# Attention outputs kept as features by tokens, two heads at a time, with probabilities scaled before they are turned

## What is computed

```python
# block 1, fox: 8 heads, causal, with a forget bias per query and key
s = einsum('qhd,khd->hqk', q, k) * scale + c_q - c_k
p = softmax(where(causal, s, -inf));  o_f = einsum('hqk,khd->qhd', p, v)
# block 1, swa: 8 heads on 2 key heads, rotary, window 128, one sink per head
p = softmax(concat([where(band, s, -inf), sink]))[..., :-1]
merged = g_f * (o_f @ w_proj_fox) + g_s * (o_s @ w_proj_swa)
# then an MoE with 64 experts (w1, w3, w2), and block 2:
# layer 0: gMLP mixer and 4 heads over 256 memory tokens; layer 1: moba (12 heads,
# here plain causal attention, as 256 tokens are one block) and 4 memory heads
x = layer_norm(ALPHA * x + concat([mix, mem_out]) @ w_mix_out)
x = layer_norm(ALPHA * x + swiglu(x))
```

## Time and profile before

| | us |
|---|---|
| median of 3 runs | 1712.14 |
| lowest and highest run | 1710.25, 1712.56 |
| span of the profiled execution | 1709.9 |
| PE busy | 1344.7 |
| DVE busy | 617.3 |
| ACT busy | 418.7 |

### The profile page before, as it was taken

One profiled execution on the slowest core, in us unless ns is written; L12 is line 12 of the kernel. 1 busy time (PEld: TensorE's weight loads), 2 busy tenths in 40 slices (PEclk: granted clock), 3 DMA queues, 4 the chain that ended last, 5 costly groups with the idle time before them and its releaser, 6 DMA issues.

```text
span 1709.9 us, 20307 instructions
## 1 busy us (share of the span) xinstructions
PE 1344.7 (79%) x8918; PEld 916.5 (54%) x8918; DVE 617.3 (36%) x821; ACT 418.7 (24%) x569; POOL 10.0 (1%) x64
## 2 busy tenths in 40 slices
PE   8999877686655656565665556689999999999998
PEld 8999724142212212221221222159888889898886
DVE  5667401001100100110011001047866676776665
ACT  5754400000000000000000000045544435444441
POOL 2000000000000000000000000000000000000000
PEclk9999989888877887877887878789999999999999
DMA  9545899999999999999999999994556655345560
GB/s 297 182 158 206 343 418 427 429 426 428 426 428 429 427 428 427 428 428 428 427 428 425 426 428 426 421 306 162 199 174 196 210 184 173 106 166 177 192 213 34
DMA packets 132233, 540.07 MB, mean 316 GB/s; under 512 B 8528, under 2 KB 90800, under 8 KB 108080
## 3 DMA queue, kind: packets, MB, share of 16 engines
q1 hardware_dynamic: 132128, 538.76, 79.6%
q10 hardware_dynamic: 16, 0.00, 0.0%
HBM read 537.69 MB, written 1.05 MB: 315 GB/s over the span
## 4 chain that ended last, share of the span: by engine, by line
PE 51%; DMA 36%; DVE 5%; ACT 4%; SPq 3%; issue 2%; DVEq 0%; ACTq 0%
DMA big<-in_w_dram 35%; PE bank L1768 9%; PE bank L2101 8%; PE bank L104 7%; PE bank L106 7%; PE bank L105 7%; PE bank L1797 4%; PE bank L2102 4%; SPq L95 3%; ACT hi_b L321 1%; DVE lo_b L335 1%; PE bank L1113 1%; PE bank L592 1%; PE bank L555 1%; PE bank L1730 1%
## 5 line engine op out<-in xcount | busy, mean ns | idle before, releaser
L1768 PE MATMUL bank<-big,xe 128*32 128x512 f32 x1984 | 284.4, 737 | 251.6 <-DMA big<-in_w_dram 251.6
L1768 PEld LDWEIGHTS bank<-big,xe 128*32 128x32 f32 x1984 | 78.1, 132 | 456.0 <-issue 456.0
L335 DVE TENSOR_TENSOR lo_b<-raw_b,hi_b 128x2048 fp32r<-128x2048 f32 x90 | 205.6, 2291 | 105.9 <-ACT hi_b L321 105.9
L1860 DVE TENSOR_TENSOR x<-bank,x 128x512 f32<-128x512 f32 x60 | 41.5, 692 | 530.1 <-PE bank L1712 530.1
L2101 PE MATMUL bank<-xT,hi_b 128*128 128x512 f32 x576 | 204.3, 398 | 0.0
L321 ACT CAST hi_b<-raw_b 128x2048 fp32r<-128x2048 f32 x91 | 172.8, 1904 | 20.4 <-PE bank L106 20.4
L1797 PE MATMUL bank<-big,gT 128*32 128x512 f32 x936 | 132.2, 716 | 54.7 <-DMA big<-in_w_dram 54.7
L2102 PE MATMUL bank<-xT,lo_b 128*128 128x256 f32 x576 | 161.7, 281 | 0.0
L2101 PEld LDWEIGHTS bank<-xT,hi_b 128*128 128x128 f32 x576 | 108.2, 188 | 26.4
L1797 PEld LDWEIGHTS bank<-big,gT 128*32 128x32 f32 x936 | 36.6, 128 | 135.9 <-issue 135.9
L2102 PEld LDWEIGHTS bank<-xT,lo_b 128*128 128x128 f32 x576 | 108.8, 189 | 0.6
(11 more groups left out here) (338 smaller groups left out, 2174.6 us busy)
## 6 DMA issues: line engine op xcount, KB each, us to landing
big<-in_w_dram SPq DMA_DIRECT2D x190, 2048.0 KB, 20.5
raw_b<-in_w_ffn_in_dram SPq DMA_DIRECT2D x44, 1024.0 KB, 5.1
raw_b<-in_w_ffn_out_dram SPq DMA_DIRECT2D x22, 1024.0 KB, 5.1
raw<-in_w_in_dram SPq DMA_DIRECT2D x15, 1024.0 KB, 9.9
raw_b<-in_b_w_in_dram SPq DMA_DIRECT2D x10, 1024.0 KB, 5.1
raw_b<-in_w_mix_out_dram SPq DMA_DIRECT2D x8, 1024.0 KB, 5.1
raw_b<-in_a_w_in_dram SPq DMA_DIRECT2D x7, 1024.0 KB, 12.8
raw<-in_w_out_dram SPq DMA_DIRECT2D x4, 1024.0 KB, 5.1
```

Source lines behind the costliest of these rows:

```text
L335: dve.tensor_tensor(self.lo[i % NRAW], self.raw[i % NRAW], self.hi[i % NH].bitcast(F32), ALU.subtract).then_inc(*self.s_lo.up(i))
L1768: last = pe.matmul(hb.t[32 * e:32 * e + 32, :], xe[:, k, 32 * e:32 * e + 32], each[e][k // 4][:, k % 4 * 512:(k % 4 + 1) * 512], start=(k ...
```

## The change

The values are the weights now (128 keys by 64 features), and the turned probabilities move (128 queries). An even head's output goes to partitions 0 to 63 and the odd head's to 64 to 127 of the same columns, in turns, so that the bank holds the output as features by tokens. The transposes of the outputs and their buffers are gone. As queries are columns there, the reciprocal of the sum can't be applied behind; instead ACT multiplies each head's probabilities (queries on partitions) by it, before PE turns them. The values are done for two units at a time, at step u+4 of the first, so the buffers of turned probabilities are 4 instead of 2. The output's bank is kept until ACT and DVE have read it. A reciprocal is taken per unit; the sink's Exp and sum too. Block 1 and block 2 use the same semaphores. Both kernels have the same score, mask, Exp and transpose instructions. Cut to its core:

```diff
 def pe_attend(pe, ps, a, ident, fill):
...
-            pe.wait_ge(*a.s_exps.of(a.base + u))
+            pe.wait_ge(*a.s_scaled.of(a.base + u))
             for i in range(0, n, P):
                 last = pe.transpose(b.t[:, i:i + P], a.p[u % 4][:, i:i + P], ident[:, :])
             last.then_inc(*a.s_p_turned.up(a.base + u))
         for go in fill.get(step, ()):
             go()
-        for job, k in a.ripe(step):
...
-            for i in range(nh // 2):
-                last = pe.transpose(b.t[:, i * P:(i + 1) * P], a.o[n % 2][:, i * P:(i + 1) * P], ident[:, :])
-            last.then_inc(*a.s_o_turned.up(n))
-        if 0 <= step - 3 < len(a.units):
-            u = step - 3
...
-                for kt in range(job.nkt):
-                    at = i * job.width + kt * P
-                    last = pe.matmul(o, a.pt[u % 2][:, at:at + P], job.value(h, kt), start=(kt == 0),
-                                     stop=(kt == job.nkt - 1))
+        if a.pair_at(step - 4):
+            two = a.pair_at(step - 4)
...
+            pe.wait_ge(*a.s_p_out.of(a.base + two[-1]))
+            each = [(h, a.pt[u % 4], i * job.width) for u in two for i, h in enumerate(a.units[u][1])]
+            for side in zip(*([x for x in each if x[0] % 2 == odd] for odd in range(2))):
+                for kt in range(job.nkt):
+                    for h, pt, at in side:
+                        last = pe.matmul(o[rows64(h % 2), h // 2 * P:(h // 2 + 1) * P], job.value(h, kt),
+                                         pt[:, at + kt * P:at + (kt + 1) * P], start=(kt == 0), stop=(kt == job.nkt - 1))
+            last.then_inc(*a.s_value.up(*(a.base + u for u in two)))
+        for u in a.ripe(step):
+            ps.let(("o", a.out_at[a.units[u][0].name]))

 def act_attend(act, ps, a, fill):
...
             last.then_inc(*a.s_exps.up(a.base + u))
+        for u in a.pair_at(step):
+            job, hs = a.units[u]
+            act.wait_ge(*a.s_share.of(a.base + u))
+            for i, h in enumerate(hs):
+                row = a.p[u % 4][:, i * job.width:(i + 1) * job.width]
+                last = act.activation(row, row, ACT.Identity, scale=job.rc[:, h:h + 1])
+            last.then_inc(*a.s_scaled.up(a.base + u))
         for go in fill.get(step, ()):
             go()

 def dve_attend(dve, ps, a, fill):
...
-            if a.base + u >= 2:
-                dve.wait_ge(*a.s_value.of(a.base + u - 2))
-            dve.tensor_copy(a.pt[u % 2][:, 0:n], ps.of(("p", a.base + u))[:, 0:n]).then_inc(*a.s_p_out.up(a.base + u))
+            if a.base + u >= 4:
+                dve.wait_ge(*a.s_value.of(a.base + u - 4))
+            dve.tensor_copy(a.pt[u % 4][:, 0:n], ps.of(("p", a.base + u))[:, 0:n]).then_inc(*a.s_p_out.up(a.base + u))
+        for u in a.pair_at(step):
+            job, hs = a.units[u]
+            sm, rc = job.sm[:, picked(hs)], job.rc[:, picked(hs)]
+            dve.wait_ge(*a.s_exps.of(a.base + u))
+            if job.sinks is not None:
+                dve.tensor_tensor(sm, sm, rc, ALU.add).then_inc(*a.s_masked.up(("sum", a.base + u)))
+                dve.wait_ge(*a.s_masked.now())
+            dve.reciprocal(rc, sm).then_inc(*a.s_share.up(a.base + u))
         for go in fill.get(step, ()):
             go()
...
-            dve.reciprocal(rc, job.sm).then_inc(*a.s_masked.up(("rc", a.base + u)))
...
-                dve.tensor_tensor(a.o[n % 2][:, 0:nh * 64].rearrange("p (h d) -> p h d", h=nh),
-                                  ps.of(("o", n))[:, 0:nh * 64].rearrange("p (h d) -> p h d", h=nh),
-                                  rc[:, h0:h0 + nh].unsqueeze(2).broadcast_to([P, nh, 64]), ALU.mult).then_inc(
-                                      *a.s_o_out.up(n))

 # ripe(step): the job's last unit u with max(u + 4, hold) == step (before: max(u + 5 + late, hold),
 # at most the number of units + 4); an extra last step is gone
 # sp_first
-        sp.wait_ge(*s["o_turned"].of(self.mix.n_out - 1))
 # act_first, fillers of fox and swa: the sigmoids go from step 11 to step 12
-        fill.update({5: [rotated], 11: [sigmoids], 13: [split], 15: [split]})
+        fill.update({5: [rotated], 12: [sigmoids], 13: [split], 15: [split]})
 # pe_last, fillers of the last attention: the second projection part goes from step 19 to step 17
-        fill.update({13: [lambda: memory_part(0)], 15: [lambda: memory_part(1)], 16: [first], 19: [first]})
+        fill.update({13: [lambda: memory_part(0)], 15: [lambda: memory_part(1)], 16: [first], 17: [first]})
```

More of the change, by code:

```diff
@@ L38 @@
 WM = 768
-PER_BANK = 8
 N_ROUNDS = S // CAP
@@ L527, in last, with pair_at, picked @@
         return hs is job.units[-1]
+    def pair_at(self, step):
+        two = range(step, min(step + 2, len(self.units)))
+        return two if step % 2 == 0 and step >= 0 else ()
     def ripe(self, step):
[L531 to L536, removed]
+        return [u for u in range(len(self.units)) if self.last(u) and max(u + 4, self.hold) == step]
+def picked(hs):
+    return slice(hs[0], hs[-1] + 1, hs[1] - hs[0])
 def pe_attend(pe, ps, a, ident, fill):
-    for step in [*a.steps(), len(a.units) + 4]:
+    for step in a.steps():
         if step % 2 == 0 and step < len(a.units):
@@ L600, in act_attend @@
[L600 to L619, removed]
+        if a.pair_at(step - 4):
+            two = a.pair_at(step - 4)
+            job = a.units[two[0]][0]
+            n = a.out_at[job.name]
+            if n not in job.opened:
+                job.opened[n] = ps.take(("o", n), a.s_o_lo, n, hold=True)
+                pe.wait_ge(*job.opened[n].was)
+            o = job.opened[n].t
+            pe.wait_ge(*a.s_p_out.of(a.base + two[-1]))
[6 more added lines that the diff above has]
+            last.then_inc(*a.s_value.up(*(a.base + u for u in two)))
@@ new lines, in pe_attend, with act_attend @@
+        for u in a.ripe(step):
+            ps.let(("o", a.out_at[a.units[u][0].name]))
+def act_attend(act, ps, a, fill):
+    for step in a.steps():
+        for u in a.pair_at(step):
+            job, hs = a.units[u]
+            nh, w = len(hs), job.width
+            p3 = a.p[u % 4][:, 0:nh * w].rearrange("p (h k) -> p h k", h=nh)
+            src = p3
+            if job.mask is None:
+                src = ps.of(("score", a.base + u))[:, 0:nh * w].rearrange("p (h k) -> p h k", h=nh)
+            act.wait_ge(*a.s_peak.of(a.base + u))
+            if u >= 4:
+                act.wait_ge(*a.s_p_turned.of(a.base + u - 4))
+            for i, h in enumerate(hs):
+                last = act.activation(p3[:, i, :], src[:, i, :], ACT.Exp, bias=job.nm[:, h:h + 1],
+                                      scale=SCALE if job.mask is None else 1.0, accum_out=job.sm[:, h:h + 1])
+            if job.sinks is not None:
+                act.wait_ge(*a.s_sink.of(a.base + u))
+                last = act.activation(job.rc[:, picked(hs)], job.rc[:, picked(hs)], ACT.Exp)
+            last.then_inc(*a.s_exps.up(a.base + u))
+        for u in a.pair_at(step):
[5 more added lines that the diff above has]
+            last.then_inc(*a.s_scaled.up(a.base + u))
@@ L620, in act_attend @@
         for go in fill.get(step, ()):
             go()
-        for job, k in a.ripe(step):
-            h0, nh = job.groups[k]
-            n = a.out_at[job.name, k]
+        for u in a.ripe(step):
+            job, _ = a.units[u]
+            n = a.out_at[job.name]
             h3, _ = pair(job.put.dst)
-            act.wait_ge(*a.s_o_turned.of(n))
-            act.copy(h3[job.put.at(h0, nh, job.qt)], ps.of(("o turned", n))[:, 0:nh * 64].rearrange(
+            act.wait_ge(*a.s_value.of(a.base + u))
+            act.copy(h3[job.put.at(0, job.heads, job.qt)], ps.of(("o", n))[:, 0:job.heads * 64].rearrange(
@@ L680, in dve_attend @@
                 dve.wait_ge(*signal.of(point))
[L681 to L701 removed]
+            dve.tensor_tensor(l3[at], ps.of(("o", n))[:, 0:job.heads * 64].rearrange("p (c s) -> p c s", s=P),
+                              h3[at].bitcast(F32), ALU.subtract).then_inc(*a.s_o_lo.up(n, (job.name, 0)))
 class Program:
```

137 lines of the change are left out of this document (49 added, 88 removed).

## The result

The kernel after takes 1719.28 us (median of 4 runs, 1717.19 to 1721.65), beside 1712.35 for the kernel before on the same chip: ratio 1.0042, 95% interval 1.003 to 1.0054. It is slower by 6.9 us, more than the 0.2% that a measurement can tell. Run once more later it took 1721.6 us beside 1711.2, ratio 1.006 (1.0043 to 1.0077). The prediction was 1717.2, slower.

A forecast was written before the change was run, and what follows sets the result against it. PE was taken to bound the attentions, a DMA stream the expert stage. Fox/swa -0.5, memory 0 +2.2 and memory 1 plus moba +3.4 gave +5.1 us on a 1709.9 span: 1715.0, so 1717.2 in whole time; range 1706 to 1723.

The forecast's parts named there:

- PE work: All attentions: 13.3 us saved on values, 3.6 on transposes, 3.2 added for shape changes; 13.7 us less in all.
- ACT work: All attentions: a scale per head, 0.40 us for 256 keys and 0.30 for 128; 26 us added in all.
- Order, which decides: All attentions: scales delay ACT's casts and evictions, then DVE's split and masks and the next Exps, so PE waits.
- Fox/swa: First attentions: PE waits 4.4 us before swa scores and 2.6 at step 12; the stream starts 0.5 us earlier.
- within 1.5 us of 175.2: Start of the expert stream: a sign that the big loads would be issued within 1.5 us of 175.2.
- From there PE bounds again with lighter steps: Fox/swa, behind the 4.4 us wait at the swa scores: PE sets the pace again, with less work per step.
- Memory 0: Memory attention 0: PE waits 3.4 us for the second pair's scales, to 1184.0; last uT pieces 2.2 us later.
- Memory 1 and moba: Last attention: k waits of 1.7, 2.2 and 2.75 us, transposes at step 16 wait too; end 3.4 us later.
- The PE saving arrives: Rival, fox/swa and moba: ACT is done when PE arrives, the whole 13.7 us come out, 1698.4; chance 0.14.
- Half the waits: Rival, mainly the last stage: without one of the small delays and fox/swa at its better end, 1709 to 1713; chance 0.18.
- Compounding: Rival, all attentions: every scale lies on the path, 26 us less 13.7 of PE gives +12.3, 1724.4; chance 0.08.
- Not two at once: Rival, value matmuls: two heads do not overlap, PE work falls by 0.4 us only, 1720; chance 0.04.

The follow-up runs named there:

- the kernel with the heads of one half first: In the kernel with the scale pass on GpSimd, value matmuls of a pair's even heads went first, odd heads behind, instead of alternating; 1707.27 us.
- the GpSimd kernel: From after, the scale pass moved from ACT to GpSimd, one multiplication by the broadcast reciprocals a unit; 1703.0 us, once more 1702.52.
- the constant transposes: From after, PE turned the identity matrix during its waits for ksT, p_b in memory 0 and kb in moba; 1719.97 us.
- the second profile of after: The kernel after, unchanged, run and profiled again on one chip with before and the GpSimd kernel; 1721.62 us, ratio 1.006.
- the pass alone on the old kernel: From before, ACT passed over every pair's probabilities once more, times 1.0, between exponentials and turning, without the new value form; 1724.74 us.

## Why the prediction was right, and where it was off

- **PE work.** Forecast 13.3 us for the values. In busy time the groups at L592 were 29.8 us (9.6 of it in the earlier trace rows) and are 16.7 at L580: 13.1. Two at once holds, by the kernel with the heads of one half first. The whole -13.7 fits the GpSimd kernel: 9.4 us faster, with 3.7 us more waits than before, which is 13.1.
- **ACT work.** Forecast 26 us, 0.40 and 0.30 each; a record is 0.50 and 0.39, the busy time 27.4, since neighbours overlap: four in a row take 1.69 us, forecast 1.6.
- **Order, which decides.** This is the step that the runs confirm most plainly: moving the same passes within ACT's queue gives 10 us back, moving them to another engine 16 to 19 in all. The part of it that said that DVE's waits for the exponentials matter was not tried by itself; that its reciprocals stand in the way of the scales made no difference that could be seen.
- **Fox/swa,** forecast -0.5 us for the start of the stream. The waits came as told (3.7 us for ksT, forecast 4.4; 2.7 for pt_a, forecast 2.6; the one for oT gone), but the big loads start at 177.31, +2.1 over the earlier trace rows, so the sign "within 1.5 us of 175.2" failed. This is the step that failed: "From there PE bounds again with lighter steps" took the full clock for granted. Behind the wait PE ran at half clock and lost 2.3 us (9.72 for 7.42). Without that the stage would be 73.8 us beside 73.6 before (an estimate from these), 0.2 us later: close to the 0.0 that the prediction's first sum gives, where the forecast was 0.5 earlier. In the three further profiles of the unchanged fox/swa stage it lost 1.6 to 2.8 us there, and in two of them another 1.6 and 2.9 behind the wait for pt_a.
- **Memory 0,** forecast +2.2, measured +2.6. The wait for the scaled second pair is 3.7 us, forecast 3.4, to 1184.58, forecast 1184.0, of which 0.3 is that the stage starts later in this profile.
- **Memory 1 and moba,** forecast +3.4, measured +3.7, though the waits are smaller than told (5.1 us for kb instead of 6.65, 1.5 at step 16 instead of 4.0, or of the 1.7 that the prediction names in brackets). Waits and end did not fit together in the prediction itself: 10.6 us of waits less 6.0 of PE work is 4.6, or 2.3 with the 1.7, and the walk ends at 3.4 between them. PE's slower stretches behind the waits for kb fill a part of the difference: with the clock kept at 1.00, the constant transposes and the waits left come to 9.7 us there (4.5 for the 37 transposes, and 5.2). The end of the stage is the same, since it was ACT's, not PE's.
- **The sum.** Forecast +5.1 us. Stages: 2.4 + 2.6 + 3.7 = 8.7, or 9.6 with the second profile of after, beside medians of +6.9 and +10.4. The miss of 2 to 5 us is mostly the clock in fox/swa. The rule on draining of the Trainium skill (TensorEngine Tiling, Key Properties) would have made PE's saving 8 us, at the price that the prediction put on a drain. The rows speak against that price: a group of 1.02 us is 0.08 more than 16 x 0.059, and the step into it is 0.21 for 0.12, 0.09 more. That is 0.17 us for the two changes of shape of a group, under the 0.2 that I had for them and far under twice 0.28.
- **Rivals.** "The PE saving arrives" is false for this kernel and true as soon as the pass leaves ACT: it gave 1698.4, measured 1702.5 to 1703.0, the rest being waits. "Half the waits" came about by reordering ACT (1709.5). "Compounding" is false for after; the nearest to it is the pass alone on the old kernel, where 60% of its busy time show. "Not two at once" is refuted.

## What to carry to other kernels

Price an operation by who is queued behind it on its engine, not by its length or by the engine's mean load. ACT at half load was the wrong place for 27 us of work, and GpSimd, where the same work took 30 us, the right one, since nothing else stood in its queue. The Trainium skill (Perfetto Trace Analysis, Optimizing GPSIMD Operations) prefers other engines because GpSimd is generally slower. The trace agrees that it is slower (30.3 us for 27.4), and yet the kernel is 16 to 19 us faster with the pass there, since the other engine's queue has work behind the pass that PE waits for. And when a saving on PE is expected and PE then waits, ask what follows the wait: work that PE itself bounds paid again here when the clock fell (1.5 to 2.9 us), work that hung on another engine did not.

## What the runs showed of the hardware

- A wait of 3.7 us on PE was followed by the lower clock level in each of the four profiles that have the unchanged one in fox/swa (mean granted clock 0.57 to 0.79 from 98 to 106 us). The wait of 2.7 us for pt_a was followed by it in three of five, one of 2.1 us for ksT in one of two. With 28 transposes of a constant in the wait of 3.7 us, the clock stayed at 1.00. The fall cost 1.5 to 2.9 us in fox/swa. In memory 0 and moba it cost nothing: these stages are equal to 0.02 us with the clock at 0.79 and 0.57 and with the clock at 1.00.
- GpSimd multiplied 128x512 by a broadcast column in 1.04 us, with DVE and ACT at work beside it. DVE's busy time is 616.5 us in that kernel and 613.4 in after; whether the two engines hold each other up was not looked into.
- The expert stream's stage differs from run to run by 4 us of 1000 for one and the same work. A change of a few us in front of it can't be read from one pair of spans; the marks of PE around memory 0 and around the last attention repeat to 0.02 us in kernels run twice, those around fox/swa to 0.9 us where the clock falls and to 0.01 where it does not.
